# Norm joints: root and reciprocal on one column per token block, spread again by a product of ones and diagonal blocks

## What is computed

```python
def _rmsnorm(x, g):
    y = xf * lax.rsqrt(jnp.mean(xf * xf, axis=-1, keepdims=True) + NORM_EPS)
    return y * g

def _sublayer(x, c, w_ada, b_ada, g_pre, g_post, fn):
    shift, scale, gate = jnp.split(silu(c) @ w_ada + b_ada, 3, axis=-1)
    h = _rmsnorm(x, g_pre) * (1 + scale) + shift
    y, aux = fn(h)
    return x + gate * _rmsnorm(y, g_post), aux
```

## Time and profile before

| | us |
|---|---|
| runs of the kernel | 2744.13, 2758.80, 2736.13 |
| median | 2744.13 |
| profiled execution | 2746.84 |
| its span, from first to last instruction | 2745.2 |
| PE busy in it | 2298.9 (84%) |
| DVE busy | 1432.7 (52%) |
| ACT busy | 872.4 (32%) |

### The profile page before, as it was taken

One profiled execution on the slowest core, in us unless ns is written; L12 is line 12 of the kernel. 1 busy time (PEld: TensorE's weight loads), 2 busy tenths in 40 slices (PEclk: granted clock), 3 DMA queues, 4 the chain that ended last, 5 costly groups with the idle time before them and its releaser, 6 DMA issues. The chain is left out here.

```text
span 2745.2 us, 64703 instructions
## 1 busy us (share of the span) xinstructions
PE 2298.9 (84%) x26373; PEld 1779.3 (65%) x26373; DVE 1432.7 (52%) x2263; ACT 872.4 (32%) x1576; POOL 346.7 (13%) x555
## 2 busy tenths in 40 slices
PE   6797788877965898769999978889778767999998
PEld 3565677766723785557777755664667655777776
DVE  2345777774237456574533354357566556554323
ACT  2335444442212222233322221137333323333222
POOL 1003233332000000101100000004111101111000
PEclk8898888987966996989999989999687788999999
DMA  7323899996364200213333323450999942232231
GB/s 241 100 74 120 281 337 333 351 351 215 92 213 141 45 4 1 79 47 88 89 85 88 90 69 115 116 162 1 270 289 286 272 129 62 71 91 85 85 93 58
DMA packets 308579, 392.58 MB, mean 143 GB/s; under 512 B 25616, under 2 KB 226650, under 8 KB 308308
## 3 DMA queue, kind: packets, MB, share of 16 engines
q1 hardware_dynamic: 276580, 282.15, 33.7%
q0 software_dynamic: 31728, 106.59, 12.1%
HBM read 377.98 MB, written 10.70 MB: 142 GB/s over the span
## 5 line engine op out<-in xcount | busy, mean ns | idle before, releaser
L816 PE MATMUL bank<-yT,WH 128*128 128x288 f16 x3200 | 535.3, 291 | 46.6 <-DVE yT L670 35.4
L816 PEld LDWEIGHTS bank<-yT,WH 128*128 128x128 f16 x3200 | 315.5, 99 | 146.5 <-issue 49.1
L880 DVE SCALAR_TENSOR_TENSOR WL<-wring,WH 128x1024 f16<-128x1024 f32 x194 | 255.3, 1320 | 271.3 <-ACT WH L860 271.2
L1252 PE MATMUL bank<-cst,kslot 128*128 128x128 f32 x1664 | 316.8, 322 | 93.4 <-DMA kslot<-in_state_dil_k 48.9
L1358 DVE TENSOR_TENSOR KL<-bank,KH 128x512 f16<-128x512 f32 x416 | 283.4, 688 | 212.4 <-ACT KH L1334 204.8
L1334 ACT CAST KH<-bank 128x512 f16<-128x512 f32 x416 | 242.7, 584 | 404.7 <-PE bank L1252 404.7
L816 PE MATMUL bank<-uT,WH 128*128 128x288 f16 x2048 | 337.6, 288 | 10.6 <-DVE WL L880 10.6
L816 PE MATMUL bank<-yT,WL 128*128 128x288 f16 x1600 | 333.6, 291 | 0.0
L860 ACT ACTIVATE WH<-wring 128x1024 f16<-128x1024 f32 x194 | 203.5, 1054 | 272.4 <-PE bank L816 220.5
L1252 PEld LDWEIGHTS bank<-cst,kslot 128*128 128x128 f32 x1664 | 207.4, 161 | 122.1 <-DMA kslot<-in_state_dil_k 55.1
L816 PEld LDWEIGHTS bank<-uT,WH 128*128 128x128 f16 x2048 | 201.5, 98 | 63.1 <-DVE WL L880 11.2
(11 more groups left out here) (431 smaller groups left out, 3576.4 us busy)
## 6 DMA issues: line engine op xcount, KB each, us to landing
kslot<-in_cache_fox_k SPq DMA_DIRECT2D x256, 256.0 KB, 5.4
vslot<-in_cache_fox_v POOLq DMA_DIRECT2D x244, 256.0 KB, 5.4
wring<-in_ada_w SPq DMA_DIRECT2D x96, 512.0 KB, 4.6
kslot<-in_state_dil_k SPq DMA_DIRECT2D x80, 512.0 KB, 12.4
vslot<-in_state_dil_v POOLq DMA_DIRECT2D x78, 512.0 KB, 12.5
wring<-in_mlp_up SPq DMA_DIRECT2D x64, 512.0 KB, 4.0
wring<-in_mlp_down SPq DMA_DIRECT2D x64, 512.0 KB, 3.9
wring<-in_ev_w_in SPq DMA_DIRECT2D x26, 512.0 KB, 3.8
```

The costliest lines, as they stand in the source:

```text
L816: last = nc.tensor.matmul(bank[b + h][:, 0:HALF], w[s % 2][:, c, :], x[:, s % parts * KC + c, h * HALF:(h + 1) * HALF], start=(s % parts = ...
L880: nc.vector.scalar_tensor_tensor(WL[s % 2][:, :, :], w[:, :, :], WSCALE, WH[s % 2][:, :, :], ALU.mult, ALU.subtract).then_inc(w_free, 1)
L1252: last = nc.tensor.transpose(b[:, j * P:(j + 1) * P], K[t % KR][:, 512 * part + j * P:512 * part + (j + 1) * P], ident)
```

## The change

Sums of squares are no longer taken with the ones as weights and the tokens streamed. `token_sums` loads 128 tokens of a chunk as weights and streams one column of ones, so that the sum of token p of block t stands in partition p, column t of one bank. Five such products cover a chunk (the fifth covers tokens 448 to 575, of which the upper 64 partitions are the new tokens). Root and reciprocal are then taken of 128x5 numbers. To bring them back over all partitions, `diagonals` multiplies the identity by each column of the reciprocals on DVE (128x512 and 128x64), and `spread_roots` multiplies ones by these diagonal blocks on PE, 64 and 512 columns wide. The result stays in PSUM, where `add_chunks` and `renorm` read it in place of `rstd`. The new tokens get one product of their own ahead of the chunks, and the chunks' products shrink from 576 to 512 columns. In the pre norm, one of DVE's two weight splits moves behind the diagonals.

```diff
+    def token_sums(pe, out, src, start, stop):
+        for t in range(NTILE + 1):
+            lo = min(t * P, TOK - P)
+            last = nc.tensor.matmul(out[:, t:t + 1], src[:, lo:lo + P], C["ones"][:, 0:1], start=start and t == 0, stop=stop and t == NTILE,
+                                    skip_group_check=True)
+        return last
+    def token_roots(act, sums, done):
+        nc.scalar.activation(std_row[:, :], sums[:, 0:NTILE + 1], ACT.Sqrt, bias=eps_rms, scale=1.0 / D).then_inc(done, 1)
+    def diagonals(dve, std_ok, inv_ok, diag_ok):
+        dve.wait_ge(std_ok, 1)
+        nc.vector.reciprocal(inv_row[:, :], std_row[:, :]).then_inc(inv_ok, 1)
+        dve.wait_ge(inv_ok, 1)
+        nc.vector.tensor_tensor(std[:, 0:NPR].rearrange("p (t n) -> p t n", n=P), ident.unsqueeze(1).to_broadcast([P, NTILE, P]),
+                                inv_row[:, 0:NTILE].unsqueeze(2).to_broadcast([P, NTILE, P]), ALU.mult).then_inc(diag_ok, 1)
+        nc.vector.tensor_scalar(std[:, NPR:TOK], ident[:, P - NDEC:P], inv_row[:, NTILE:NTILE + 1], None, ALU.mult).then_inc(diag_ok, 1)
+    def over_tokens(banks):
+        return banks[1][:, 0:NPR], banks[0][:, NDEC:2 * NDEC]
+    def spread_roots(pe, banks, diag_ok, done):
+        prompt, sample = over_tokens(banks)
+        pe.wait_ge(diag_ok, 2)
+        nc.tensor.matmul(sample, C["ones"], std[:, NPR:TOK], start=True, stop=True)
+        nc.tensor.matmul(prompt, C["ones"], std[:, 0:NPR], start=True, stop=True).then_inc(done, 1)
+    def add_chunks(dve, banks, spread, scaled, added):
+        prompt, sample = over_tokens(banks)
+        dve.wait_ge(spread, 1)
+        nc.vector.tensor_tensor(yT[:, :, NPR:TOK], yT[:, :, NPR:TOK], sample.unsqueeze(1).to_broadcast([P, KC, NDEC]), ALU.mult).then_inc(scaled, 1)
         for k in range(KC + 1):
             if k < KC:
-                nc.vector.tensor_tensor(yT[:, k, :], yT[:, k, :], rstd[:, :], ALU.mult).then_inc(scaled, 1)
+                nc.vector.tensor_tensor(yT[:, k, 0:NPR], yT[:, k, 0:NPR], prompt, ALU.mult).then_inc(scaled, 1)
             if k:
-                dve.wait_ge(scaled, k)
+                dve.wait_ge(scaled, k + 1)
                 nc.vector.tensor_tensor(xT[:, k - 1, :], xT[:, k - 1, :], yT[:, k - 1, :], ALU.add).then_inc(added, 1)
 
...
             if root_known:
                 return
+            if add:
+                spread_roots(pe, bank[4:6], diag1, spread1)
             for k in range(KC):
                 pe.wait_ge(squared, k + 1)
-                last = ones_sums(pe, bank[6:8], hT[:, k, :], k == 0, k == KC - 1)
+                last = token_sums(pe, bank[6], hT[:, k, :], k == 0, k == KC - 1)
             last.then_inc(sum2, 1)
+            spread_roots(pe, bank[6:8], diag2, spread2)
 
         def on_act(act, splits):
             if add:
-                roots(act, bank[4:6], std1)
+                token_roots(act, bank[4], std1)
             splits()
             if not root_known:
                 for k in range(KC):
@@ -634,7 +675,7 @@
                         act.wait_ge(added, k + 1)
                     nc.scalar.activation(hT[:, k, :], xT[:, k, :], ACT.Square).then_inc(squared, 1)
                 act.wait_ge(sum2, 1)
-                roots(act, bank[6:8], std2)
+                token_roots(act, bank[6], std2)
             act.wait_ge(smp, 3)
...
             if add:
-                inverse(dve, std1, inv1)
-                add_chunks(dve, scaled, added)
+                diagonals(dve, std1, inv1, diag1)
+                add_chunks(dve, bank[4:6], spread1, scaled, added)
                 dve.wait_ge(added, KC)
             nc.vector.tensor_tensor(seqs(yT[:, :, late]), seqs(xT[:, :, late]), of_seq(A), ALU.mult).then_inc(smp, 1)
-            splits()
+            splits((0,))
             if not root_known:
-                inverse(dve, std2, inv2)
+                diagonals(dve, std2, inv2, diag2)
+            splits((1,))
+            if not root_known:
+                dve.wait_ge(spread2, 1)
             dve.wait_ge(smp, 1)
-            nc.vector.tensor_tensor(hT[:, :, late], yT[:, :, late], rstd[:, late].unsqueeze(1).to_broadcast([P, KC, NDEC]), ALU.mult).then_inc(smp, 1)
+            nc.vector.tensor_tensor(hT[:, :, late], yT[:, :, late], root_sample.unsqueeze(1).to_broadcast([P, KC, NDEC]), ALU.mult).then_inc(smp, 1)
 
             def unit(k):
-                nc.vector.scalar_tensor_tensor(hT[:, k, 0:NPR], xT[:, k, 0:NPR], mod[:, A + k, 0:1], rstd[:, 0:NPR], ALU.mult, ALU.mult).then_inc(u_ok, 1)
+                nc.vector.scalar_tensor_tensor(hT[:, k, 0:NPR], xT[:, k, 0:NPR], mod[:, A + k, 0:1], root_prompt, ALU.mult, ALU.mult).then_inc(u_ok, 1)
 
...
         def after_pe(pe):
             pe.wait_ge(acc_ok, KC)
-            ones_sums(pe, bank[4:6], acc, True, False)
+            token_sums(pe, bank[4], acc, True, False)
             pe.wait_ge(sq_a, KC)
             pe.wait_ge(sq_d, 2 * KC)
-            ones_sums(pe, bank[4:6], sq, False, True)
+            token_sums(pe, bank[4], sq, False, True)
 
...
-                    roots(act, bank[4:6], std1)
+                    token_roots(act, bank[4], std1)
...
-                    inverse(dve, std1, inv1)
-                    add_chunks(dve, scaled, added)
+                    diagonals(dve, std1, inv1, diag1)
+                    add_chunks(dve, bank[4:6], spread1, scaled, added)
                     dve.wait_ge(added, KC)
 
                 @block.tensor
                 def _(pe):
+                    spread_roots(pe, bank[4:6], diag1, spread1)
```

More of the change, by code:

```diff
@@ L210, in build_trunk @@
     rstd = sb(top, "rstd", [P, TOK])
+    std_row, inv_row = (sb(top, n, [P, NTILE + 1]) for n in ("std_row", "inv_row"))
     scT = sb(top, "scT", [P, KC, 32])
@@ L596, in inverse @@
         dve.wait_ge(done, 2)
-    def add_chunks(dve, scaled, added):
+    def token_sums(pe, out, src, start, stop):
[24 more added lines that the diff above has]
+        nc.vector.tensor_tensor(yT[:, :, NPR:TOK], yT[:, :, NPR:TOK], sample.unsqueeze(1).to_broadcast([P, KC, NDEC]), ALU.mult).then_inc(scaled, 1)
         for k in range(KC + 1):
             if k < KC:
-                nc.vector.tensor_tensor(yT[:, k, :], yT[:, k, :], rstd[:, :], ALU.mult).then_inc(scaled, 1)
+                nc.vector.tensor_tensor(yT[:, k, 0:NPR], yT[:, k, 0:NPR], prompt, ALU.mult).then_inc(scaled, 1)
             if k:
-                dve.wait_ge(scaled, k)
+                dve.wait_ge(scaled, k + 1)
                 nc.vector.tensor_tensor(xT[:, k - 1, :], xT[:, k - 1, :], yT[:, k - 1, :], ALU.add).then_inc(added, 1)
@@ L610, in renorm @@
         high, rest = split_views(yT)
-        std1, inv1, scaled, added, squared, sum2, std2, inv2 = (
-            sem(n) for n in ("std1", "inv1", "scaled", "added", "squared", "sum2", "std2", "inv2"))
+        std1, inv1, diag1, spread1, scaled, added, squared, sum2, std2, inv2, diag2, spread2 = (
+            sem(n) for n in ("std1", "inv1", "diag1", "spread1", "scaled", "added", "squared", "sum2", "std2", "inv2", "diag2", "spread2"))
+        root_prompt, root_sample = (rstd[:, 0:NPR], rstd[:, NPR:TOK]) if root_known else over_tokens(bank[6:8])
         smp, high_s, rest_s, u_ok, high_ok, rest_ok, whole_ok = (sem(n) for n in ("smp", "high_s", "rest_s", "u_ok", "high_ok", "rest_ok", "whole_ok"))
@@ L775, in one, with splits @@
                         extra[s](eng, done)
-                def splits():
-                    split(0, 0)
-                    split(0, 1)
+                def splits(units=(0, 1)):
+                    for s in units:
+                        split(0, s)
                 if before:
@@ L2555, in add_and_store @@
     def add_and_store():
-        std1, inv1, scaled, added, turned, row_a, smp_a = (sem(n) for n in ("std1", "inv1", "scaled", "added", "turned", "row_a", "smp_a"))
+        std1, inv1, diag1, spread1, scaled, added, turned, row_a, smp_a = (
+            sem(n) for n in ("std1", "inv1", "diag1", "spread1", "scaled", "added", "turned", "row_a", "smp_a"))
         with ExitStack() as sc:
```

## The result

The changed kernel took 2782.75 us as the median of 4 runs (2774.46 to 2786.32), beside 2747.82 for 4 runs of the kernel before: 1.0109 times as long, 95% interval 1.0069 to 1.0150. Put beside the kernel before a second time, the ratio was 1.0087 (1.0056 to 1.0119). So the change makes the kernel about 1% slower, 30 us by the first ratio (19 to 41) and 24 by the second (15 to 33). Forecast were +17 us, 2761, in a range that ended at 2774: the direction and the mechanism held, the size didn't.

What follows compares the result with a forecast made beforehand. PE was taken to bound the kernel, its trunk sums holding up the joints. Three joints at +17.9 us (slower sums +19.9, conversions and earlier start -2.0) and -0.6 in the last gave 2744.1 + 17.3 = 2761.4 us, range 2739 to 2774.

Steps and rivals of the forecast that it cites:

- What bounds a joint, and which clock: In the joints, PE's sums hold up the second conversion; half clock for all trunk sums and the spreads beside them.
- rival A: In the pre norm's sums, the clock rises 5.8 us in as before; median 2742 us; chance 0.13.
- The trunk's sums: Pre norm's 80 one-column instructions on PE, 0.214 us apart at half clock: 17.3 us in place of 10.85, 10.41 and 10.23.
- The conversion: Root, reciprocal, diagonals and spread in each norm: 3.65 us at half clock against 4.33, saving 0.68 each.
- The first products behind a joint: Next projection's first products start at 0.50 as before; a shift of the clock's rise was taken as 0.
- The post norm's sums and the additions: In each joint, the post norm's sums cost nothing more; DVE's additions cost +0.47 us up to the first square.
- The sum: Three joints at +17.9 us together and the last at -0.6: +17.3 us for the run.
- The range: Whole run's median: from 2739 us to 2774, the upper end of the pace and the scatter of a median.
- Slower by over 1%: Whole run slower by more than 27.4 us, from 2771.5: chance 0.08 together.
- B: Through the joints, the clock stays up after the post norm's spread: 13.2 us less, 2731; chance 0.07.
- C: In the trunk's sums, one-column products don't overlap the next load: 0.38 us apart, +57 us, 2801; chance 0.05.
- D: In the joints, reads of PSUM slow DVE by 0.05 us each: +2.8 us; only shifts the others, no own chance.

Runs made afterwards that it cites:

- the run that had both clocks in one joint: The changed kernel with idle PE time in the joints filled by products nobody reads: 2794.58 us, 1.0149 times the kernel before.
- post norms only: The changed kernel with the pre norm given back its old form: 2750.64 us, 0.9991 times the kernel before.
- before with f16 squares: The kernel before, with the trunk's squares and the ones that sum them in f16: 2754.70 us, 1.0013 times the kernel before.
- the repeat: The changed kernel measured once more without an edit: 2775.72 us, 1.0087 times the kernel before.

## Why the prediction was wrong, and where it was right

- **What bounds a joint, and which clock.** Right in what came. PEclk was 0.50 in all of the trunk's sums and in the spreads, and PE was what the second root waited for. That the clock is the cause of the slow sums is shown by the run that had both clocks in one joint. The rows that I set against rival A show one side only. The same trace has the other, in the columns of the earlier trace rows, with one of the products of the first stretch:

```profile
1022.00:1024.00 2.00, 2.00 (x76) 1.00 0.04 8
1022.68 1.10 PE L1940 MATMUL bank<-hT,p 64*64 64x64 f32 x32
1834.00:1837.00 3.00, 3.00 (x28) 1.00 1.04 400
```

From 903 to 1028 us nearly all of PE's products have 64x64 loads, as in the row at 1030 to 1046, and PEclk is 1.00 throughout. In the second stretch line 330's 24 products of 18 columns stayed at 1.00 as well. So the rows left open which clock the new sums would get, and that it was the half one is in part luck.
- **The trunk's sums.** 17.3 us forecast, 17.22 measured, 0.214 from one instruction to the next.
- **The conversion.** Forecast 3.65, measured 3.97, so it saves 0.36 and not 0.68. Short were the root (0.27 for 0.20), the diagonals of the new tokens (0.25 for 0.19) and the spread (2.5 for 2.32; here 128x128 weights, where the row I took had 64x64; that this is the reason isn't shown). Over six conversions that is 1.9 us more than in my sum for the three joints (20.1 measured, 17.9 forecast). The last joint saved 0.3 for my 0.6, up to its last addition.
- **The first products behind a joint.** Taken as 0; they took 0.8 us more in all (43.0 for 42.2 from first product to third split). This is no clear effect of the change: two other kernels in which this part is unchanged, post norms only and before with f16 squares, also took 0.7 more. With the conversions it makes 2.7; the sums' 3 x 0.08 and rounding take 0.5 back.
- **The post norm's sums and the additions.** Nothing and +0.47 forecast; 1.25 for 1.21 us, and +0.46. Right.
- **The sum.** 17.3 forecast; the joints and the end together cost 19.8. This was a small miss, and most of it is the conversion's price.
- **The range.** This is the step that failed. It added 17.3 to the median of three runs, 2744.1, as if that were exact, and its upper end left 13 us above the forecast for the pace of the sums and the scatter of one median. Over 24 runs the kernel before has its median at 2752, 8 us higher. 2752 + 20 = 2772 would have been inside; 2782.75 isn't. The 11 us that are left lie in no term of the sum, and their cause stays open: on the repeat, 2775.72, 4 are left. Ahead of the first joint alone two profiles of the changed kernel differ by 12 us, and I had written down the runs' spread, 2736 to 2759, without giving it room in the range.
- **The chances.** Slower by over 1% had 0.08. The two measured ratios lie on either side of that line (1.0109 and 1.0087), with intervals that hold it, so the size of the loss was rated too surely.
- **Rivals.** A and B fell with the clock; C fell with 0.214 us apart; D with products of 0.68 us that read PSUM, as before. By the rule of the Trainium skill that I had weighed ("TensorE: Matmul & The Clock Gate", "What's actually happening"), unbroken matmuls would bring the clock up; 17.2 us of unbroken one-column matmuls did not, so the measurement decides against that reading.

## What to carry to other kernels

Here a product of one column cost its weight load. So turning a sum round, so that the data are the weights, pays only if the loads are cheap (here f16, not f32) or hidden. Before moving work to PE in a stretch where it idles, ask at which clock it will run there: ten of these products took 1.28 us at one clock and 2.13 at the other, within one joint. Read the clock from all rows of the nearest shape, also from those that speak against the guess. And give the range the scatter that the runs show, that of its own starting point too, not only the scatter of the sum's terms.

## What the runs showed of the hardware that was not expected

- 128x128 loads of f16 with one column each went 0.03 us apart at the half clock, those of f32 0.214, and f32 needs two to a call: 0.43 us for a block of 128 tokens against 0.06 (five calls in 0.29).
- PE can be busy without a gap, with products of 256 f32 columns ahead of every chunk's sums from the second on, and the granted clock still falls, from 1.00 to 0.50 during the second chunk's sums, 2.3 us after the first chunk's began.
- With one unread product of 384 columns ahead of the second spread and five behind it, the next projection started at 2.4 GHz. Its first product to the third weight split then took 1.4 to 2.5 us less a joint than in the same kernel without them, for work that nobody reads.
